# The forget gate's row sums on all partitions: sixteen one-hot matmuls replaced by a DMA through a DRAM scratch

## What is computed

```
proj = h @ w_in                       # conv parts cb, cc, cin; q, k, v; f_logit (8 heads); gates g
u = causal_dwconv(cc * cin, conv_mix_w)
y_conv = (cb * u) @ w_out_conv
log_f = log_sigmoid(f_logit + b_f)
F = cumsum(log_f, axis=1).transpose(0, 2, 1)            # [head, token]
s = q @ k^T * scale + F[query] - F[key]                 # per head, causal
o = softmax(s) @ v
gates = sigmoid(g_logit + b_gate)
x = x + (g_conv * y_conv + g_attn * (o @ w_out_attn)) @ w_o
```

## Time and profile before

| | us |
|---|---|
| median of 3 timed runs | 1411.95 |
| lowest and highest of them | 1409.2, 1412.6 |
| profiled execution | 1405.81 |
| its span, first to last instruction | 1404.1 |
| PE busy | 1372.3 (98%) |
| DVE busy | 779.8 (56%) |
| ACT busy | 514.6 (37%) |
| POOL busy | 92.5 (7%) |

### The profile page before, as it was taken

How to read it: one execution, slowest core, us unless ns; L and a number is a source line. 1 busy time by engine, 2 the same in 40 slices (tenths; PEclk the granted TensorE clock), 3 DMA queues, 4 the chain that set the end, 5 groups by cost and what they waited for, 6 DMA issues and landing times.

```text
span 1404.1 us, 15788 instructions
## 1 busy us (share of the span) xinstructions
PE 1372.3 (98%) x6294; PEld 1081.3 (77%) x6294; DVE 779.8 (56%) x887; ACT 514.6 (37%) x583; POOL 92.5 (7%) x81
## 2 busy tenths in 40 slices
PE   7999999999999999997999999999999999999997
PEld 5777667688888889995877788657878888888886
DVE  7786545843333357876435433555766666674232
ACT  5453562422121235454211332454343344332122
POOL 4001000200000011233000000000310000000000
PEclk9999999999999999999999999999999999999999
DMA  5322001123332359541322222200323232223131
GB/s 163 118 90 90 31 1 56 62 93 98 102 98 90 119 139 266 104 100 47 119 91 90 90 90 90 90 1 31 107 74 119 66 113 90 90 91 119 60 105 60
DMA packets 103172, 128.24 MB, mean 91 GB/s; under 512 B 3298, under 2 KB 80338, under 8 KB 103122
## 3 DMA queue, kind: packets, MB, share of 16 engines
q1 hardware_dynamic: 97282, 115.99, 25.2%
q0 software_dynamic: 5824, 11.54, 4.6%
q10 hardware_dynamic: 16, 0.00, 0.0%
HBM read 125.43 MB, written 2.10 MB: 91 GB/s over the span
## 4 chain that ended last, share of the span: by engine, by line
PE 89%; DVE 4%; issue 3%; POOL 2%; ACT 1%; DMA 0%; ACTq 0%; SPq 0%; DVEq 0%; POOLq 0%
PE psum L1488 25%; PE psum L1486 25%; PE psum L1487 25%; PE psum L1608 3%; PE psum L1620 2%; PE psum L1632 2%; PE psum L1824 2%; DVE w_lo L904 2%; POOL tmp L560 1%; PE psum L1757 1%; PE psum L1758 1%; PE psum L1759 1%; ACT w_hi L584 1%; DVE act_lo L913 1%; PE psum L1836 1%
## 5 line engine op out<-in xcount | busy, mean ns | idle before, releaser
L1486 PE MATMUL psum<-act_hi,w_hi 128*128 128x512 f32 x1224 | 487.8, 399 | 13.1 <-DVE act_lo L913 6.5
L1488 PE MATMUL psum<-act_hi,w_lo 128*128 128x512 f32 x1224 | 487.5, 398 | 0.0
L1487 PE MATMUL psum<-act_lo,w_hi 128*128 128x512 f32 x1224 | 482.8, 394 | 0.0
L584 ACT ACTIVATE w_hi<-raw 128x2048 fp32r<-128x2048 f32 (+1 forms) x102 | 192.5, 1887 | 611.9 <-PE psum L1488 599.8
L904 DVE TENSOR_TENSOR w_lo<-raw,w_hi 128x2048 fp32r<-128x2048 f32 (+1 forms) x102 | 233.8, 2292 | 127.0 <-ACT w_hi L584 126.9
L1486 PEld LDWEIGHTS psum<-act_hi,w_hi 128*128 128x128 f32 x1224 | 230.1, 188 | 78.5 <-issue 15.6
L1487 PEld LDWEIGHTS psum<-act_lo,w_hi 128*128 128x128 f32 x1224 | 230.3, 188 | 58.3 <-issue 1.4
L1488 PEld LDWEIGHTS psum<-act_hi,w_lo 128*128 128x128 f32 x1224 | 230.2, 188 | 54.3
L1757 PE MATMUL psum<-part_hi,w_hi 128*128 128x256 f32 x308 | 87.2, 283 | 0.9
L1758 PE MATMUL psum<-part_lo,w_hi 128*128 128x256 f32 x308 | 87.0, 282 | 0.0
L1759 PE MATMUL psum<-part_hi,w_lo 128*128 128x256 f32 x308 | 86.9, 282 | 0.0
(11 more groups left out here) (256 smaller groups left out, 1551.9 us busy)
## 6 DMA issues: line engine op xcount, KB each, us to landing
raw<-in_w_in SPq DMA_DIRECT2D x30, 1024.0 KB, 5.2
raw<-in_w_ffn_in SPq DMA_DIRECT2D x22, 1024.0 KB, 5.1
raw<-in_w_up SPq DMA_DIRECT2D x22, 1024.0 KB, 5.1
raw<-in_w_down SPq DMA_DIRECT2D x10, 1024.0 KB, 5.1
x_buf<-in_w_ffn_out POOLq DMA_DIRECT2D x6, 1024.0 KB, 10.7
raw<-in_w_out SPq DMA_DIRECT2D x4, 1024.0 KB, 5.1
raw<-in_w_o SPq DMA_DIRECT2D x4, 1024.0 KB, 5.1
x_buf<-in_w_ffn_out POOLq DMA_DIRECT2D x3, 768.0 KB, 10.7
```

The lines of the kernel that those rows point to most:

```text
L584: A(w_hi[:, s % 2, 0:n], home(s, n), ACT.Copy).then_inc(w_hi_ready, 1)
L1486: mm(dst, stationary[0], moving[0], start=first, stop=False)
L1487: mm(dst, stationary[0], moving[1], start=False, stop=False)
L1488: return mm(dst, stationary[1], moving[0], start=False, stop=last)
```

## The change

The row sums go to all partitions by two DMAs that POOL issues: `fsum[:, 0]` (8 x 512) is stored to a scratch tensor `f_rows` in DRAM, and when that has landed, the whole scratch is read back as one row of 4096 values onto each of 128 partitions, straight into `neg_f`. VectorE waits for that once, before head 0. ScalarE waits for the store before it writes the first gate, since the gates later overwrite `fsum`. The one-hot matmuls, their operands `f_split` and `ident_r`, the copies and all their semaphores go.

```
-        ident_r = sb("ident_r", [HEADS, HEADS], F32R)
...
-        f_split = sb("f_split", [HEADS, 2, TOKENS], F32R, inner)
...
+        f_rows = nc.dram_tensor("f_rows", (HEADS, TOKENS), F32, kind="Internal").ap()
...
# POOL
-            g.tensor_copy(ident_r[:], ident[0:HEADS, 0:HEADS]).then_inc(const_bf, 1)
...
+                if rs[0] == N_FINAL:
+                    pool.wait_ge(f_sum, 1)
+                    g.dma_start(f_rows, fsum[:, 0]).then_inc(f_stored, 16)
+                    pool.wait_ge(f_stored, 16)
+                    every = f_rows.rearrange("(a h) n -> a (h n)", a=1).broadcast_to([P, HEADS * TOKENS])
+                    g.dma_start(neg_f[:].rearrange("p h n -> p (h n)"), every).then_inc(negf_in, 16)
# ScalarE
-                if S_CC <= s < S_CC + HEADS:
-                    h = s - S_CC
-                    act.wait_ge(negf_done, h + 1)
-                    A(neg_f[:, h], psum[:, bank_of(GROUP[s]) + 3], ACT.Copy).then_inc(negf_ready, 1)
+                if s == S_GC:
+                    act.wait_ge(f_stored, 16)
# VectorE
-                    dve.wait_ge(f_sum, 1)
-                    V.tensor_copy(f_split[:, 0], fsum[:, 0]).then_inc(f_parts, 1)
-                    dve.wait_ge(f_parts, 1)
-                    V.tensor_tensor(f_split[:, 1], fsum[:, 0], f_split[:, 0].bitcast(F32), ALU.subtract).then_inc(f_parts, 1)
...
-                dve.wait_ge(negf_ready, h + 1)
+                if h == 0:
+                    dve.wait_ge(negf_in, 16)
# PE
-                    pe.wait_ge(const_bf, 6)
+                    pe.wait_ge(const_bf, 5)
...
-                if s == S_OC2:
-                    pe.wait_ge(negf_ready, HEADS)
...
-                if S_CC <= s < S_CC + HEADS:
-                    h = s - S_CC
-                    pe.wait_ge(f_parts, 2)
-                    if h == 0:
-                        wait_freed(GROUP[S_V2])
-                    if h >= 2:
-                        pe.wait_ge(negf_ready, h - 1)
-                    row = ident_r[:, h:h + 1].broadcast_to([HEADS, P])
-                    mm(psum[:, bank_of(GROUP[s]) + 3], row, f_split[:, 0], start=True, stop=False)
-                    mm(psum[:, bank_of(GROUP[s]) + 3], row, f_split[:, 1], start=False, stop=True).then_inc(negf_done, 1)
```

More of the change, by code:

```diff
@@ L383, in two_blocks @@
         ms2_ready, f_pre, f_exp, f_ln, f_sum = sem("ms2_ready"), sem("f_pre"), sem("f_exp"), sem("f_ln"), sem("f_sum")
-        f_parts = sem("f_parts")
-        negf_done, negf_ready = sem("negf_done"), sem("negf_ready")
+        f_stored, negf_in = sem("f_stored"), sem("negf_in")
         gate_pre, gate_ready = sem("gate_pre"), sem("gate_ready")
```

## The result

| | before, us | after, us |
|---|---|---|
| median of the timed runs | 1410.58 (4 runs) | 1386.49 (4 runs) |
| lowest and highest | 1409.03, 1412.60 | 1384.12, 1389.16 |
| profiled execution | 1405.81 | 1387.45 |
| its span | 1404.1 | 1385.7 |

The ratio is 0.9829 with an interval of 0.9804 to 0.9854: the change saves 24.1 us, 1.7%. The forecast was 6.8 us less, and the range ended at 1399.5 us. The sign was right, and the time fell 13 us outside the range. One execution of the kernel before that ran beside four of the later versions took 3440.8 us; the ratios leave this slow run out.

The account below looks back on a forecast made before the run. TensorE (PE), busy 98% of the span, was taken to bound the kernel. Terms of -6.8 us for the pairs and 0 for everything else gave 1411.95 - 6.8 = 1405.1 us, range 1399.5 to 1409.5 us.

Parts of the forecast that it names:

- PE bounds the kernel, and a boundary has no gap of its own: TensorE, busy 98% of the span, sets the time; slab boundaries without a pair keep the usual 0.23 us step.
- 0.85 us a pair, 6.8 us in all, all of it on the path: Eight slabs with a one-hot pair take 12.05 us each, against 11.20 without; removing the pairs saves 6.8 us.
- Rival (a): At the pairs, only the columns' time goes and the idle loader stays: 3.7 us saved, 1408.2 us; chance 5%.
- rival (b): Gain hidden by VectorE losing over 1.9 us more per slab or by a late load: 1412 us; chance 8%.
- The stretch bears the pace: In the former pair slabs, partners keep up; VectorE's idle after convolutions falls from 2.73 to 1.9 us, nothing taken back.
- Evictions and split at 0: Removing the eight ScalarE copies to neg_f and VectorE's two small f_split operations gains 0 us, as both engines idle afterwards.
- The two DMAs at 0: POOL's store of the row sums and 2 MB broadcast cost 0 us, landing long before neg_f is read at 890.3.
- The block of 3 MB: Sign: DMA engines busy from about 702 in one block, broadcast plus weight load, with that load landing by 718.
- Rival (c): The broadcast starves the weight load issued at 704.46, so PE waits: slower, up to 1422.6 us; chance 4%.
- The 32 bytes at 0: Removing ident_r moves every tile behind it in SBUF by its 32 bytes per partition; priced at 0 us.
- Rival (d): More than the sum, some us from moved tiles or a stall elsewhere that goes: 1399 us or less; chance 2%.
- The profiled run against the median: Forecast taken from the timed median, 1411.95 us, some 6 us above the profiled execution of 1405.8 us.

Follow-up runs that it names:

- distance 0: 192 bytes of padding in front of gain_both: kernel before, with ident_r also moved to the top of SBUF, 1380.84 us; changed kernel 1373.69 us.
- distance 96: act_hi's place less w_hi's, modulo 256 bytes, in the kernel before (1410.58 us) and in the changed kernel with 32 bytes of padding (1403.29 us).
- distance 64: Placement of the changed kernel (1386.49 us); with pairs, the kernel before with only ident_r moved behind all tiles, 1388.93 us, ratio 0.9863.

## Why the prediction was wrong, point by point

- **PE bounds the kernel, and a boundary has no gap of its own:** right. In the kernel after, the last matmul of the first cc slab starts at 714.45 in PE's time line, and the first two of the next slab at 714.69 and 714.92, nearly as in the earlier trace rows. The idle loader of the earlier trace rows is gone.
- **0.85 us a pair, 6.8 us in all, all of it on the path:** right. 96.40 - 89.60 = 6.80 us. The change with the tiles kept in place gained 6.1 us, and at distance 0 the pairs cost 7.04 us. Rival (a), the columns alone at 3.7 us, and rival (b), a hidden gain, did not come.
- **The stretch bears the pace:** right. VectorE idled 1.88 us where 1.9 was forecast and 2.73 stood before, by its time line in the kernel after:

```profile
743.75 2.86 DVE L1305 SCALAR_TENSOR_TENSOR conv_u<-conv_p,par,conv_u 128x511 f32<-128x511 f32 x4
748.49 1.29 DVE L1262 TENSOR_TENSOR tmp<-psum,rstd 128x512 f32<-128x512 f32 x2 [1.88 <-PE psum L1487]
```

- **Evictions and split at 0:** nothing speaks against it. The change alone gained 6.1 us, no more than the pairs.
- **The two DMAs at 0:** right, and their durations were put too high. POOL took 0.6 us for an issue (1.3 were taken from its accumulating loads), the store 1.8 us (3.0), the broadcast 7.6 us (10.4). It landed sooner than its value by the slab's rate, and far from the 39.6 us bound. The block of 3 MB did not form as foreseen, since the broadcast had nearly landed when the next load started. Rival (c), the starved load, did not come.
- **The 32 bytes at 0: this step failed.** It said: "PE streams w_hi (in front of it) up to 710.88 and act_hi (behind it) from 711.11 on at one pace, so I price that at 0." The rows are right, but two neighbouring starts give one step, not the pace of a slab, and they show one placement (distance 96). Even there the paces are not quite equal: the trace of before has 11.25 us for the value slab that ends there, and 11.20 for the cc slab behind it. And from two equal paces at one placement nothing would follow for another. In fact the move was worth more than the change: 20.4 us alone, against 6.1 for the change alone. The 0.05 us a slab could have told that the pace depends on which tile streams; it gave no price for a move. The step's worth should have been left with a bound of its own, and the range should have been widened for it. A slab at the later 10.88 us, by contrast, could not have been guessed from before at all.
- **Rival (d)** was the one that came: more than the sum, from tiles that moved. Its chance of 2% and its "some us" were both too small. The cause was written down, and its price was not worked out.
- **The profiled run against the median:** the addition was made from the median, 6 us above the profiled run, and that was right. The gain by the spans alone would be 18.4 us in place of 24.1.

The 24 us are not a sum of two independent terms (6.1 and 20.4 would give 26.5). The pairs at distance 64 also acted as breaks. With them, the fifteen slabs from the first cc on run at the short step in between, and without them at the long one, which costs the changed kernel 3.0 us (171.48 - 168.45). 20.4 + 6.8 - 3.0 = 24.2.

**What stays open.** Why the distance sets the step is not shown: the runs give a pattern with a period of 256 bytes, not a mechanism. Nor is it shown why, at distance 64, the long step stays on after w_hi has been streamed until something odd comes between, and why single executions had the long step in a stretch where others had the short. Distances that are no multiple of 32 bytes were not tried, and 224 only with w_hi streamed at 32. Nor was a distance of its own for each pair of tiles. The products stage, which streams other tiles, took 98.4 us at distances 0 and 96, 96.3 to 97.1 at 64 and 95.4 at 192, so the best for it is not the best for the slabs.

## What to carry to other kernels

Whoever removes or adds a small tile moves every tile behind it. Before a change gets the credit, run it once with the tile's bytes kept as padding, and compare the step of the same matmuls in a stretch that the change does not touch. Where PE is busy for 98% of the span, try the distance between the streamed and the stationary tiles as a size of its own; here 192 bytes of padding were worth another 10 to 17 us by the two ratios (0.9758 and 0.9705 against 0.9829). In a forecast, a side effect that no row can price is not zero: it belongs into the range with both signs.

## What was not expected of the hardware

- The step of 512-column matmuls at the granted clock 1.00 depends on how far apart in a partition the two operands start. By the start of the streamed tile less that of the stationary one, modulo 256 bytes, it is 0.2267 us at 0, 0.2289 or 0.2333 at 64, 0.2323 or 0.2333 at 128, 0.2344 at 160, and 0.2333 at 32, 96, 192 and 224. The best to the worst differ by 3.4%.
- The Trainium skill ("TensorE: Matmul & The Clock Gate", Back-to-back issue gap) gives about 216 ns for an isolated step of this width, and about 131 ns a matmul in a stream of weight loads and matmuls. These runs are such streams, and the best of them has 226.7 ns.
- At one and the same placement the step can hold one of two values for over 150 us. It differs between executions of one kernel, and in the stretch where one column of another matmul was put in front, it was 10.99 us a slab in place of 11.20.
- A pair of 8-row matmuls between full ones costs 0.85 to 0.88 us, nearly twice its 0.47 us of columns.
- The attention's granted clock differs between runs of one kernel (0.94 to 1.00), and its length with it, in steps of some 1.5 us. That is as large as many a change.
